# Folding 1/rms into the activations: from the first recurrence iteration to the second convolution iteration of a hybrid decoder block

## The reference, cut to what matters

```
u      = x * rsqrt(mean(x*x) + eps) * norm_w                     # 256 x 4096
a_q, a_f, a_i, a_g, c_b, c_c, c_h, c_g, g_a, g_b = split(u @ w_in)  # 8 pieces of 2048 columns, 2 of 4096
y_a    = rmsnorm(recurrence(a_q, sigmoid(a_f), a_i)) * hgrn_norm_w * silu(a_g)   # 16 heads
y_b    = (c_b * conv3(c_c * c_h)) * silu(c_g)
merged = sigmoid(g_a + bias0) * (y_a @ w_branch_a) + sigmoid(g_b + bias1) * (y_b @ w_branch_b)
out    = rmsnorm(x + merged @ w_out) * final_norm_w
```

## Time and profile before

| | us |
|---|---|
| median of 3 runs (lowest, highest) | 2910.14 (2909.88, 2911.77) |
| the profiled execution's own time | 2909.99 |
| its span from the first to the last instruction | 2908.0 |
| PE busy | 2862.8 |
| DVE busy | 1883.7 |
| ACT busy | 1303.0 |

### The profile page before, as it was taken

One profiled execution on the slowest core, in us unless ns is written; L12 is line 12 of the kernel. 1 busy time (PEld: TensorE's weight loads), 2 busy tenths in 40 slices (PEclk: granted clock), 3 DMA queues, 4 the chain that ended last, 5 costly groups with the idle time before them and its releaser, 6 DMA issues.

```text
span 2908.0 us, 39267 instructions
## 1 busy us (share of the span) xinstructions
PE 2862.8 (98%) x12989; PEld 2370.6 (82%) x12989; DVE 1883.7 (65%) x2056; ACT 1303.0 (45%) x1364; POOL 7.9 (0%) x23
## 2 busy tenths in 40 slices
PE   8899999999999999999999999999999999899998
PEld 7688888888888888888878888888888888688886
DVE  6866666666665545555569687786867768555454
ACT  5443444344434444444445454454545545344443
POOL 1000000000000000000000000000000000000000
PEclk9999999999999999999999999999999999999999
DMA  7455555555555556565556666666666666566665
GB/s 238 149 171 175 173 179 169 176 172 176 173 174 184 190 190 194 189 192 188 188 182 201 210 217 207 204 210 193 217 203 221 199 213 204 206 196 213 218 202 202
DMA packets 428993, 564.06 MB, mean 194 GB/s; under 512 B 25617, under 2 KB 287874, under 8 KB 428930
## 3 DMA queue, kind: packets, MB, share of 16 engines
q1 hardware_dynamic: 428930, 563.25, 60.2%
HBM read 555.28 MB, written 7.86 MB: 194 GB/s over the span
## 4 chain that ended last, share of the span: by engine, by line
PE 95%; DVE 3%; DMA 1%; ACT 1%; issue 0%; DVEq 0%; SPq 0%; ACTq 0%
PE PS L1103 24%; PE PS L1105 23%; PE PS L1104 23%; PE QL L1231 5%; PE QL L1232 5%; PE QL L1233 5%; PE PS L1231 2%; PE PS L1232 2%; PE PS L1233 2%; PE QL L1134 2%; DVE QS L617 1%; PE QL L1111 1%; DVEq L596 0%; ACT QS L387 0%; DMA RP<-in_w_in 0%
## 5 line engine op out<-in xcount | busy, mean ns | idle before, releaser
L617 DVE TENSOR_TENSOR QS<-RP,QS 128x1024 fp32r<-128x1024 f32 x800 | 975.9, 1225 | 886.6 <-ACT QS L387 873.8
L387 ACT ACTIVATE QS<-RP 128x1024 fp32r<-128x1024 f32 x800 | 845.9, 1059 | 1255.8 <-PE PS L1105 1154.2
L1103 PE MATMUL PS<-QS,U 128*128 128x512 f32 x2560 | 1009.5, 394 | 15.7 <-DVE QS L617 15.7
L1105 PE MATMUL PS<-QS,U 128*128 128x512 f32 x2560 | 998.7, 390 | 0.0
L1104 PE MATMUL PS<-QS,U 128*128 128x512 f32 x2560 | 997.8, 390 | 0.0
L1103 PEld LDWEIGHTS PS<-QS,U 128*128 128x128 f32 x2560 | 481.9, 188 | 115.0 <-DVE QS L617 15.2
L1105 PEld LDWEIGHTS PS<-QS,U 128*128 128x128 f32 x2560 | 481.5, 188 | 101.3
L1104 PEld LDWEIGHTS PS<-QS,U 128*128 128x128 f32 x2560 | 482.1, 188 | 97.0
L1231 PE MATMUL QL<-QS,U 128*128 128x512 f32 x688 | 267.9, 389 | 0.0
L1232 PE MATMUL QL<-QS,U 128*128 128x512 f32 x688 | 267.7, 389 | 0.0
L1233 PE MATMUL QL<-QS,U 128*128 128x512 f32 x688 | 267.7, 389 | 0.0
(11 more groups left out here) (215 smaller groups left out, 1873.8 us busy)
## 6 DMA issues: line engine op xcount, KB each, us to landing
RP<-in_w_in SPq DMA_DIRECT2D x1024, 256.0 KB
RP<-in_w_in SPq DMA_DIRECT2D x256, 512.0 KB
RP<-in_w_out SPq DMA_DIRECT2D x128, 512.0 KB
RP<-in_w_branch_a SPq DMA_DIRECT2D x64, 512.0 KB
RP<-in_w_branch_b SPq DMA_DIRECT2D x64, 512.0 KB
XS<-in_x SPq DMA_DIRECT2D x8, 512.0 KB, 5.5
XR<-in_x SPq DMA_DIRECT2D x8, 512.0 KB, 4.6
out_dram<-H SPq DMA_DIRECT2D x8, 512.0 KB, 3.9
```

The source lines that it names most:

```text
L387: act.activation(WS[s][:, :, 0:OW], RAW[s][:, :, :], ACT.Copy).then_inc(hi_ready, 1)
L617: dve.tensor_tensor(WS[s][:, :, OW:2 * OW], RAW[s][:, :, :], WS[s][:, :, 0:OW], ALU.subtract).then_inc(lo_ready, 1)
L1103: pe.matmul(bank, top, w[:, k, 0:OW], start=at_k == 0, stop=False)
L1105: op = pe.matmul(bank, low, w[:, k, 0:OW], start=False, stop=at_k == n_tiles - 1)
```

## The change: what it does

1/rms is applied to the drained results in all recurrence iterations and in the first convolution iteration, and U is scaled in place in the second convolution iteration, in eight batches of four k-tiles, so that its group 1 is the first that multiplies a scaled U. In the last merge iteration, PE's transposes come after chunks 3, 5, ..., 15, ACT's and DVE's parts of them after their chunks 6, 8, ..., 18, and SP's reloads stand at chunks 3, 9, 11, 13 in place of 4, 6, 8, 10.

```diff
-NORM_BATCHES = ((0, 8), (8, 16), (16, 24), (24, 28), (28, 32))
+NORM_TILES = 4
+NORM_AT = {5: 0, 6: 1, 8: 2, 9: 3, 10: 4, 11: 5, 12: 6, 13: 7}
...
@@ SP, merge
-                        if last and at_c >= 4 and at_c % 2 == 0:
-                            for m in ((0, 1, 2, 3) if at_c == 4 else (at_c // 2 + 1,) if at_c < 12 else ()):
+                        if last:
+                            for m in {3: (0, 1, 2, 3), 9: (4,), 11: (5,), 13: (6,)}.get(at_c, ()):
...
@@ ACT, branch (norm_hi now takes U[:, 4n:4n+4])
-                    if first and slot in (11, 13, 15):
-                        norm_hi((slot - 11) // 2)
+                    if norm and slot - 1 in NORM_AT:
+                        norm_hi(NORM_AT[slot - 1])
...
-                        act.activation(CSF[:, :, :], PS[0][:, :, T:2 * T], ACT.Sigmoid).then_inc(gate_c, 1)
+                        for b in range(2):
+                            scale = inv_rms(b) if scaled or norm else 1.0
+                            op = act.activation(CSF[:, b, :], PS[0][:, b, T:2 * T], ACT.Sigmoid, scale=scale)
+                        op.then_inc(gate_c, 1)
...
-                if first:
-                    norm_hi(3)
-                    norm_hi(4)
...
-                    if last and c >= 7 and c % 2 == 1 and c < 2 * CB + RING + 1:
-                        turned_hi((c - 7) // 2)
+                    if last and c >= 6 and c % 2 == 0:
+                        turned_hi((c - 6) // 2)
...
@@ DVE
+            def rms_diagonal():
+                dve.memset(ONES[:, :], 1.0)
                 for b in range(2):
                     op = dve.tensor_scalar(DG[:, b * P:(b + 1) * P], IDN[:, :], inv_rms(b), None, ALU.mult)
                 op.then_inc(rms_ready, 1)
...
             def norm_scale(n):
-                a, b = NORM_BATCHES[n]
-                t = NT[n % 2][:, 0:b - a, :]
-                dve.wait_ge(w_used, CD + (b + 1) // KC)
+                k = slice(NORM_TILES * n, NORM_TILES * (n + 1))
+                t = NT[n % 2][:, :, :]
+                dve.wait_ge(w_used, CONV_CHUNK + BRANCH + NORM_TILES * (n + 1) // KC)
...
@@ DVE, branch, in this order behind lo of the slot's two chunks
-                    if first and slot in (10, 12, 14):
-                        norm_scale((slot - 10) // 2)
-                    if first and slot in (11, 13, 15):
-                        norm_lo((slot - 11) // 2)
+                    if a is not None:
+                        attention(a, slot)
+                    if norm and slot == 1:
+                        rms_diagonal()
+                    if norm and slot == 4:
+                        dve.wait_ge(rms_spread, 1)
+                        dve.tensor_copy(RB[:, :], OB[:, 0:T])
+                    if norm and slot in NORM_AT:
+                        norm_scale(NORM_AT[slot])
+                    if norm and slot - 1 in NORM_AT:
+                        norm_lo(NORM_AT[slot - 1])
...
+                                for b in range(2):
+                                    dve.scalar_tensor_tensor(CF[:, b, :], PS[0][:, b, T:2 * T], inv_rms(b),
+                                                             CSF[:, b, :], ALU.mult, ALU.mult)
...
-                            take(GA, PS[0], first).then_inc(drained, 1)
+                            scaled(GA, PS[0]).then_inc(drained, 1)
...
-                if first:
-                    norm_scale(3)
-                    norm_lo(3)
-                    norm_scale(4)
-                    norm_lo(4)
...
@@ PE, group: normed is now group 1 of the second convolution iteration
-                        for n, (a, _) in enumerate(NORM_BATCHES):
-                            if a == KC * c:
-                                pe.wait_ge(u_norm, n + 1)
+                        pe.wait_ge(u_norm, KC * c // NORM_TILES + 1)
...
@@ PE, branch
-                    if first and c == CD + 1:
-                        pe.wait_ge(consts, 7)
-                        pe.wait_ge(rms_ready, 1)
-                        pe.matmul(SC[0][:, 0:T], ONES[:, :], DG[:, :], start=True, stop=True).then_inc(rms_spread, 1)
...
+                    if norm and c == CONV_AT + 1:
+                        pe.wait_ge(rms_ready, 1)
+                        pe.matmul(OB[:, 0:T], ONES[:, :], DG[:, :], start=True, stop=True).then_inc(rms_spread, 1)
...
-                    if last and c % 2 == 0 and c >= 2 * CD + 2:
-                        n = (c - 2 * CD - 2) // 2
+                    if last and c % 2 == 1 and c >= 2 * CD + 3:
+                        n = (c - 2 * CD - 3) // 2
```

More of the change, by code:

```diff
@@ L102, in build @@
         MB = [at(f"MB{i}", [P, 2, OW], region_v + i * 2 * OW * 4) for i in range(4)]
-        NT = [at(f"NT{i}", [P, 8, T], region_y + i * 8 * T * 4) for i in range(2)]
+        NT = [at(f"NT{i}", [P, NORM_TILES, T], region_m + i * NORM_TILES * T * 4) for i in range(2)]
+        ONES = at("ONES", [P, P], region_m + 2 * NORM_TILES * T * 4)
+        DG = at("DG", [P, T], region_m + 2 * NORM_TILES * T * 4 + 4 * P)
+        RB = at("RB", [P, T], region_m + 2 * NORM_TILES * T * 4 + 4 * P + 4 * T)
         FW = at("FW", [P, D], region_m)
@@ L362, in _ @@
             pool.memset(KL[:, :, :], 0.0).then_inc(consts, 1)
-            pool.memset(ONES[:, :], 1.0).then_inc(consts, 1)
-            pool.wait_ge(consts, 7)
+            pool.wait_ge(consts, 6)
             for n, m in enumerate(LEVELS[:6]):
@@ L436, in seven_hi, with branch @@
                 act.activation(U[:, 0:N_SEVEN, P:T], XT[:, 2, :, :], ACT.Copy).then_inc(v_hi, 1)
-            def branch(i, chunk0, a=None, first=False, is_conv=False, last=False):
+            def branch(i, chunk0, a=None, first=False, is_conv=False, norm=False, scaled=False, last=False):
                 for slot in range(SLOTS):
@@ L471, in branch @@
                         act.wait_ge(drained, CONV_GROUP + 2 * i + 1)
-                        act.activation(CSF[:, :, :], PS[1][:, :, 0:T], ACT.Copy).then_inc(gate_c, 1)
-                if first:
-                    norm_hi(3)
-                    norm_hi(4)
+                        for b in range(2):
+                            op = act.activation(CSF[:, b, :], PS[1][:, b, 0:T], ACT.Copy, scale=inv_rms(b) if scaled else 1.0)
+                        op.then_inc(gate_c, 1)
             branch(0, 0, first=True)
@@ L479, in _ @@
                 branch(i, 0, a=i - 1)
-            branch(0, CONV_CHUNK, a=NP - 1, is_conv=True)
-            with act.Fori(1, NP - 1) as i:
+            branch(0, CONV_CHUNK, a=NP - 1, is_conv=True, scaled=True)
+            branch(1, CONV_CHUNK, is_conv=True, norm=True)
+            with act.Fori(2, NP - 1) as i:
                 branch(i, CONV_CHUNK, is_conv=True)
@@ L846, in scaled, with branch @@
                 return op
-            def take(dst, src, first):
-                return scaled(dst, src) if first else dve.tensor_copy(dst[:, :, :], src[:, :, :])
-            def branch(i, chunk0, a=None, first=False, is_conv=False, conv_of=None, last=False):
+            def branch(i, chunk0, a=None, first=False, is_conv=False, conv_of=None, norm=False, unscaled=False, last=False):
                 for slot in range(SLOTS):
@@ L873, in branch @@
                         seven_lo()
-                    if a is not None:
-                        attention(a, slot)
                     if conv_of is not None and 2 <= slot < 5:
@@ L882, in branch @@
                             dve.wait_ge(gate_c, 2 * i + 1)
-                            dve.tensor_tensor(CF[:, :, :], PS[0][:, :, T:2 * T], CSF[:, :, :], ALU.mult)
-                            after()
-                            dve.tensor_tensor(CF[:, :, :], PS[0][:, :, 0:T], CF[:, :, :], ALU.mult).then_inc(drained, 1)
+                            if unscaled:
+                                dve.tensor_tensor(CF[:, :, :], PS[0][:, :, T:2 * T], CSF[:, :, :], ALU.mult)
+                                after()
+                                op = dve.tensor_tensor(CF[:, :, :], PS[0][:, :, 0:T], CF[:, :, :], ALU.mult)
+                            else:
+                                for b in range(2):
+                                    dve.scalar_tensor_tensor(CF[:, b, :], PS[0][:, b, T:2 * T], inv_rms(b),
+                                                             CSF[:, b, :], ALU.mult, ALU.mult)
+                                after()
+                                for b in range(2):
+                                    op = dve.scalar_tensor_tensor(CF[:, b, :], PS[0][:, b, 0:T], inv_rms(b),
+                                                                  CF[:, b, :], ALU.mult, ALU.mult)
+                            op.then_inc(drained, 1)
                         else:
-                            take(GA, PS[0], first).then_inc(drained, 1)
+                            scaled(GA, PS[0]).then_inc(drained, 1)
                         after()
@@ L896, in branch @@
                             dve.wait_ge(gate_c, 2 * i + 2)
```

(35 more changed lines are left out.)

24 lines of the change are left out of this document (9 added, 15 removed).

## The result

The changed kernel takes 2932.64 us (median of 4 runs, 2931.12 to 2934.78) against 2910.01 of the kernel before in the same set: a ratio of 1.0078, 95% interval [1.0061, 1.0096]. It is slower by 22.6 us; the forecast was 23.5 us, 2933.6.

A forecast was written before the change was run, and what follows sets the result against it. PE, busy 98% of the span, was taken as the bound. Gains 14.0 + 15 = 29.0 against losses 4.1 + 35.8 + 12.6 = 52.5 gave net 23.5 us slower, 2933.6 us; 8-in-10 range 2922 to 2946.

The forecast's parts named there:

- First iteration, 14.0 us gained: First iteration's end and second's start: without batches, PE's waits and slow stretch go; 14.0 us gained, bounds 11.3 and 14.5.
- Last merge, 15 us gained: Last merge iteration's 16 chunks: PE's waits for turned_lo and most half clock go; 15 us gained, bounds 10 and 16.3.
- The feared wait of 1.3 us for chunk 4: Last merge: reloads ahead of chunk 4's load might make PE wait 1.3 us, or not if it lands 1.7 earlier.
- the second mechanism: Last merge before the change: SP's reload of block 4 blocks a weight load, issued 6.9 us after the issue before.
- (a): Second convolution iteration, spreading 1/rms: PE waits 3.1 us for DG before the ONES product, plus 1.0 half-clock charge; 4.1 lost.
- (b): Second convolution iteration, batches: PE idles five times 6.26 us, once 3.66, and 0.8 for batch 0; 35.8 us lost.
- (c): Half clock behind the six large gaps of the second convolution iteration: 2.1 us each, 12.6 lost; bounds 0 and 28.8.
- The rival with full clock throughout (2920): Second convolution iteration: gaps come but slow stretches don't, 2920 us; chance 0.08.
- half clock throughout: Rival: whole bursts between gaps at half clock, 28.8 us in place of 12.6, and 2.2 in (a); 2951 us; chance 0.10.
- Costed at nothing: Split drains of iterations 2 to 8, halved convolution activations, scalar operands: hidden in slots 7 and 15; uncovered, 10 us.
- a short gap is free of that: PE's clock: a 1.81 us gap leaves the next matmul at 0.47 us, so no half clock follows.
- The rival that would have made it faster (2886): norm_lo of batches 2 to 7 done before PE ends chunk 2n+15, so scaling is hidden: 2886 us; chance 0.06.

The follow-up runs named there:

- the two kernels with and without it: Kernel before with only the last merge iteration's part of the change, 2894.72 us; changed kernel without DG, ONES product and batches, 2880.15 us.
- the reloads alone: Kernel before with only SP's reloads moved to chunks 3, 9, 11, 13 in the last merge iteration: 2906.85 us, ratio 0.9987.
- the order alone: Kernel before with last-merge transposes one chunk later, turned_hi and turned_lo one chunk earlier, SP's reloads unmoved: 2895.53 us, ratio 0.995.
- Moving the diagonal: Changed kernel with the diagonal made in slot 15 of the first convolution iteration, ONES product after chunk 1 of the second: 2928.71 us, ratio 1.0064.
- the filled kernel: Changed kernel with 20 unused matmuls (10 for the last batch) ahead of PE's wait for each of batches 2 to 7: 2921.28 us, ratio 1.0037.
- the kernel without batches: Changed kernel without DG, ONES product and all batches, so U is never scaled: 2880.15 us, ratio 0.9898.
- The spread-out kernel: Changed kernel with early diagonal and ONES product, batches at slots 2, 4, 5, 6, 8, 9, 10, 12, norm_lo ahead of norm_scale: 2880.97 us.
- `norm_lo` first: Changed kernel with norm_lo of the batch before set ahead of norm_scale in DVE's slot: 2920.07 us, ratio 1.0034.
- earlier slots: Changed kernel with batches at slots 4, 5, 7 to 12 in place of 5, 6, 8 to 13: 2893.01 us, ratio 0.9939.

## Why the prediction was right, point by point

- **First iteration, 14.0 us gained.** 13.9 to 14.6 by the two kernels with and without it. In the changed trace the wait behind `x_rms` is 0.65 us where it was 1.01.
- **Last merge, 15 us gained.** 15.6, the upper part of the bounds. The feared wait of 1.3 us for chunk 4 didn't come, by a margin of about 0.2 us; the reloads alone show that it was real. Of the two mechanisms that the prediction named for the old waits, the order of `turned_lo` carries the gain. With the order alone, SP's reloads still block weight loads as before, and PE waits for none of them, so the second mechanism, which the prediction called worse, was not a cost. Its number was misread too: the row before the reload holds two issues, 2484.10 and 2.39 us long, so the reload went out 4.5 us behind their end, not 6.9.
- **(a), 4.1 us lost.** The wait was 2.87, not 3.1: the memset and the diagonal took 0.44 us together, since they overlap (894.48 to 894.92), not 0.63. The half clock behind it, charged by half, was absent in the profiled run. Moving the diagonal gave 3.9 by the medians. The bound of 2.2 for the half clock was too low: two of the other kernels had 6.0 and 6.4 us of it there, 3 us lost.
- **(b), 35.8 us lost.** 34.7 + 0.83 = 35.5: five gaps of 6.22 (6.26 forecast), one of 3.60 (3.66), and 0.83 at chunk 16 (0.8).
- **(c), 12.6 us lost.** 11.4 by filling the gaps, and about 11 by comparing the bursts of the two traces. The prediction took 2.1 for each of six gaps; it was 2.2 behind the first, falling to 1.7 behind the fifth, and about 1.5 behind the shorter sixth. The rival with full clock throughout (2920) is what the filled kernel brought about; half clock throughout did not come, since it ended 4.8 to 3.7 us into the first five bursts of 8.0 to 7.5 us. The Trainium skill's figure for a burst (1.67 us throttled; "TensorE: Matmul & The Clock Gate", section "HAM oscillation — how this bites in real kernels") would have given an estimate of 0.8 per gap. This trace agrees with its pattern, that each burst behind such a wait pays, and not with its size.
- **Costed at nothing.** The new drains cost nothing that a trace shows: the recurrence iterations are as long as before (96.6 to 96.7 us), and so are the later convolution iterations (87.97).
- **In no term.** Each gap also costs some 0.3 us at its two ends: at full clock throughout, the filled kernel's bursts still take 5.75 us (950.24 to 955.99), where 24 matmuls without a gap take 5.44. Over the six gaps that is about 1.9 us.

The sum was 52.5 lost; the iteration's length says 52.1, and the kernel without batches 52.5 or 52.2. The mechanism was right in each part, but that the total agrees so closely is in part luck: the terms (a) to (c) came out at about 49.4 in the profiled run (2.9, 35.5 and 11), and the ends of the gaps, which the prediction did not count, make up most of the rest. The gains were low by 0.5 to 1.2 us, and the runs themselves spread by 3 to 4 us.

The rival that would have made it faster (2886) decided at chunk 20, as it said. The spread-out kernel is this rival come true: DVE had the time, 77.5 of 96 us; only its place in the order was wrong.

## What to carry to other kernels

When work is moved into an in-order engine's idle time, ask what the instruction ahead of it waits for. If that is the end of the consumer's last step before the one that needs the work, no idle time hides any of it, and the whole chain becomes a gap, each time; here two chunks of lead turned 34.7 us of such waits into 4.1, and spreading the batches out left none. And a gap in front of dense matmuls can cost more than its length: a third more where it was 6.2 us (1.7 to 2.2), and about half more where it was 3.6 to 3.8 (some 11.5 for 21.8), in half clock behind it. Making such a gap shorter does not give back the second price as long as the clock still falls.

## What the runs showed of the hardware

**The same gap did and didn't cost clock.** The wait of 2.87 or 2.88 us ahead of the ONES product is in four kernels. In the changed kernel and the one with `norm_lo` first, the product behind it took 0.70 us. In the one with earlier slots and the one with filled gaps it took 1.22:

```profile
896.22 1.22 PE L1228 MATMUL QL<-DG,ONES 128*128 128x256 f32 x2 [2.88 <-DVE DG L653]
```

```profile
896.00:900.00 4.00, 3.78 (x9) 3.02 (x10) 0.17 (x1) 0.00 (x0) 0.00 (x0) 0.50 0.43 133
```

(Both rows, one of the timeline and one of the windows, are of the kernel with earlier slots.) So around 3 us one trace doesn't tell whether a gap costs clock. The gaps of 6.2 us always did, and the five of 1.69 us in the filled kernel never did. But the kernel before has a gap of nearly that size that did, 10 us behind its gap of 4.41:

```profile
2511.42 0.66 PE L1172 MATMUL QL<-IDN,MB 128*128 128x128 f32 x4 [1.94 <-DVE U L985]
```

```profile
2512.00:2515.20 3.20, 3.20 (x12) 2.62 (x11) 0.50 (x1) 0.00 (x0) 0.00 (x0) 0.51 0.40 137
```

The prediction's "a short gap is free of that" rested on one gap of 1.81 us and does not hold for this one. Of its sum only the half charge in (a) leaned on it.

**The clock can fall after PE is at work again.** In the kernel with `norm_lo` first, PE starts behind a gap of 3.83 us at full clock, and its matmuls drop to half over a microsecond later:

```profile
943.37 0.50 PE L1120 MATMUL PS<-QS,U 128*128 128x512 f32 x1 [3.83 <-DVE U L670]
...
944.40 0.39 PE L1121 MATMUL PS<-QS,U 128*128 128x512 f32 x1
944.63 0.52 PE L1122 MATMUL PS<-QS,U 128*128 128x512 f32 x1
944.95 0.63 PE L1120 MATMUL PS<-QS,U 128*128 128x512 f32 x1
```

It was so behind three of that kernel's six gaps, and behind the 2.77 us gap of the kernel with earlier slots. A first matmul at full speed therefore does not show that a gap was free; the granted clock of the whole burst does.
